# Down product of the sample rows: high and low halves of z in one stationary of 64 columns, and their units first in each group of the second block

## What is computed

```python
def ffn(h, w_up, w_down):
    return jnp.square(jax.nn.relu(h @ w_up)) @ w_down

xp = xp + ffn(rmsnorm(xp, norm_ffn_g[l]), w_up[l], w_down[l])
xs = xs + ffn(rmsnorm(xs, norm_ffn_g[l]), w_up[l], w_down[l])
...
y_prompt = rmsnorm(xp, norm_f_g)
y_sample = rmsnorm(xs, norm_f_g)
```

## Time and profile before

| | |
|---|---|
| median of 3 runs | 2716.34 us (2716.27 to 2719.45) |
| profiled execution | 2719.28 us, span 2717.6 us |
| mean granted clock of PE | 0.963 of full speed |
| busy | PE 2524.3, PEld 2268.7, DVE 1409.3, ACT 699.8, POOL 272.8 us |

### The profile page before, as it was taken

One profiled execution on the slowest core, in us unless ns is written; L12 is line 12 of the kernel. 1 busy time (PEld: TensorE's weight loads), 2 busy tenths in 40 slices (PEclk: granted clock), 3 DMA queues, 4 the chain that ended last, 5 costly groups with the idle time before them and its releaser, 6 DMA issues.

```text
span 2717.6 us, 36622 instructions
## 1 busy us (share of the span) xinstructions
PE 2524.3 (93%) x13872; PEld 2268.7 (83%) x13872; DVE 1409.3 (52%) x2411; ACT 699.8 (26%) x1421; POOL 272.8 (10%) x533
## 2 busy tenths in 40 slices
PE   5899999995699996489999999998799999999997
PEld 3799999995588885279898989897689888888986
DVE  5245654683566664454545454445544454445445
ACT  5223332211333431132121212123312121121212
POOL 4000011000333330210000000003400000000002
PEclk9999999997799997689999999999799999999999
DMA  4123334314455532232121111111312111111201
GB/s 140 42 71 99 102 113 124 114 62 146 143 148 147 141 111 69 85 117 62 32 62 31 62 34 59 41 52 40 116 32 62 31 46 46 46 46 31 62 23 70
DMA packets 212761, 208.03 MB, mean 77 GB/s; under 512 B 30251, under 2 KB 184043, under 8 KB 209322
## 3 DMA queue, kind: packets, MB, share of 16 engines
q1 hardware_dynamic: 212658, 206.63, 25.0%
HBM read 156.91 MB, written 49.79 MB: 76 GB/s over the span
## 4 chain that ended last, share of the span: by engine, by line
PE 53%; POOL 2%; issue 1%; ACT 1%; DMA 0%; DVE 0%; SPq 0%; DVEq 0%; POOLq 0%; ACTq 0%
PE bank L122 18%; PE bank L124 18%; PE bank L123 18%; ACT f_relu L140 0%; DMA f_up_raw<-in_w_up_dram 0%; PE bank L177 0%; POOL f_acc L1603 0%; POOL f_acc L1601 0%; POOL fn_rs L111 0%; POOL ff_rt L109 0%; POOL fn_ms L145 0%; POOL ff_rt L108 0%; POOL fn_rt L109 0%; POOL fn_rt L108 0%; POOL fn_rt L110 0%
## 5 line engine op out<-in xcount | busy, mean ns | idle before, releaser
L1710 DVE TENSOR_TENSOR f_acc<-bank,f_acc 128x512 f32<-128x512 f32 x512 | 353.2, 691 | 320.5 <-PE bank L124 319.9
L122 PE MATMUL bank<-f_h_hi,f_up_lo 128*128 128x344 f32 (+1 forms) x1536 | 494.3, 322 | 4.3 <-DVE f_up_lo L1705 2.2
L124 PE MATMUL bank<-f_h_hi,f_up_hi 128*128 128x344 f32 (+1 forms) x1536 | 492.6, 321 | 0.0
L123 PE MATMUL bank<-f_h_lo,f_up_hi 128*128 128x344 f32 (+1 forms) x1536 | 492.6, 321 | 0.0
L122 PE MATMUL bank<-f_dn_hi,f_z_lo 128*128 128x512 f32 x1088 | 432.8, 398 | 0.5 <-ACT f_relu L1638 0.5
L124 PE MATMUL bank<-f_dn_hi,f_z_hi 128*128 128x512 f32 x1088 | 429.6, 395 | 0.0
L123 PE MATMUL bank<-f_dn_lo,f_z_hi 128*128 128x512 f32 x1088 | 428.4, 394 | 0.0
L122 PE MATMUL bank<-h_hi,w_lo 128*128 128x412 f32 (+3 forms) x1000 | 352.7, 353 | 1.9 <-DVE w_lo L667 1.9
L123 PE MATMUL bank<-h_lo,w_hi 128*128 128x412 f32 (+3 forms) x1000 | 351.5, 352 | 0.0
L124 PE MATMUL bank<-h_hi,w_hi 128*128 128x412 f32 (+3 forms) x1000 | 351.1, 351 | 0.0
L122 PEld LDWEIGHTS bank<-f_h_hi,f_up_lo 128*128 128x128 f32 x1536 | 291.3, 190 | 7.7 <-DVE f_up_lo L1705 2.5
(11 more groups left out here) (326 smaller groups left out, 2918.1 us busy)
## 6 DMA issues: line engine op xcount, KB each, us to landing
f_up_raw<-in_w_up_dram SPq DMA_DIRECT2D x64, 512.0 KB, 4.8
f_dn_raw<-in_w_down_dram SPq DMA_DIRECT2D x64, 512.0 KB, 3.4
p_dram<-y SPq DMA_DIRECT2D x24, 1024.0 KB, 4.7
w_raw<-in_w_in_dram SPq DMA_DIRECT2D x24, 512.0 KB, 5.3
xres<-in_x_prompt_dram SPq DMA_DIRECT2D x16, 512.0 KB, 4.7
x_dram<-x SPq DMA_DIRECT2D x16, 512.0 KB, 3.1
f_acc<-x_dram SPq DMA_DIRECT2D x16, 512.0 KB, 4.8
out_y_prompt_dram<-f_acc SPq DMA_DIRECT2D x16, 512.0 KB
```

The costliest lines, as they stand in the source:

```text
L122: pe.matmul(out, wl, xh, start=start and k == 0, stop=False, skip_group_check=skip)
L123: pe.matmul(out, wh, xl, start=False, stop=False, skip_group_check=skip)
L124: last = pe.matmul(out, wh, xh, start=False, stop=stop and k == n - 1, skip_group_check=skip)
L1710: dve.tensor_tensor(dst, bank, dst, ALU.add).then_inc(s["y_added"], 1)
```

## The change

The stationary of the sample rows becomes `z_sample`, 64 columns wide for each j: columns 0 to 7 are the high part, columns 32 to 39 the low part, and the others are zero. One matmul (`both`) multiplies all 64 columns with the high part of `w_down`; a second one (`high`) multiplies the first 32 columns with its low part. So the unit's bank holds the high part's products in partitions 0 to 7 and the low part's in 32 to 39. DVE adds 64 partitions to an accumulator of 64 rows, `s_acc`. After the last group ACT moves rows 32 to 39 to `s_low`, DVE adds them to rows 0 to 7, and the rows are squared, scaled and stored. The two sample units are now the first two of each group of the second block. POOL makes their scales ahead of those of the prompt tiles. At the start of `ffn`, ACT zeroes the padding and saves the rows, DVE zeroes `s_acc`, and ACT puts the rows back. DVE makes `z_lo` of the sample columns with an instruction of its own.

```diff
...
-    z_hi = sb("z_hi", [P, GH, W], F32R)
-    z_lo = sb("z_lo", [P, GH, W], F32R)
+    z = sb("z", [P, GH, 2 * (BLK + PAD)], F32R)
+    z_hi, z_sample, z_lo = z[:, :, 0:W], z[:, :, BLK:BLK + 2 * PAD], z[:, :, BLK + 2 * PAD:]
+    s_acc = c.x_s_room
...
+    final_s = Stats(c, st, "ffs_", xn[:, 1, :])
+    s_low = xn[0:n, 0, :]
...
     def units(blk):
-        out = [(u, slice((u // 2) * P, (u // 2 + 1) * P), u % 2, psum[ZB + u % ZB][:, :],
-                slot(blk, u // 2)[:, (u % 2) * 512:(u % 2 + 1) * 512]) for u in range(2 * NBT)]
-        if blk == 1:
-            out += [(u, slice(BLK, W), u % 2, psum[ZB + u % ZB][0:n, :], c.x_s[:, (u % 2) * 512:(u % 2 + 1) * 512])
-                    for u in range(2 * NBT, UNITS[1])]
+        before = 2 * blk
+        out = sample_units() if blk == 1 else []
+        out += [(u + before, slice((u // 2) * P, (u // 2 + 1) * P), u % 2, psum[ZB + (u + before) % ZB][:, :],
+                 slot(blk, u // 2)[:, (u % 2) * 512:(u % 2 + 1) * 512]) for u in range(2 * NBT)]
         return out
+    def sample_units():
+        return [(u, None, u, psum[ZB + u][0:2 * PAD, :], s_acc[:, u * 512:(u + 1) * 512]) for u in range(2)]
...
+            eng.wait_ge(s["s_final"], 1)
+            eng.dma_start(io["y_sample"].rearrange("b s d -> (b s) d"), s_acc[0:n, :]).then_inc(s["s_stored"], 16)
             for m in range(NBT):
                 eng.wait_ge(stored[m % 2], 16 * (NBT // 2 + m // 2))
                 store_rows(1, m)
...
+            final_s.scales(pool, 0, 0, 1, NS)
             for pair in range(NBT // 2):
                 finals[1].scales(pool, pair, 2 * pair)
-            finals[1].scales(pool, NBT // 2, NBT, 1, NS)
...
+            act.activation(z_sample, heads(c.ident[:], GH), ACT.Copy, scale=0.0).then_inc(s["z_padded"], 1)
+            act.activation(s_low, c.x_s[:], ACT.Copy).then_inc(s["s_saved"], 1)
+            act.wait_ge(s["s_zeroed"], 1)
+            act.activation(c.x_s[:], s_low, ACT.Copy).then_inc(s["s_placed"], 1)
...
+            act.wait_ge(s["y_added"], outputs_before(1, NG - 1) + 3)
+            act.activation(s_low, s_acc[PAD:PAD + n, :], ACT.Copy).then_inc(s["low_moved"], 1)
+            act.wait_ge(s["s_summed"], 1)
+            final_s.square(act, 0, 0, s_acc[0:n, :], NS)
             for m in range(NBT):
                 finished_square(1, m)
...
+                        if cols.stop > BLK:
+                            ends = slice(BLK, W)
+                            dve.tensor_tensor(z_sample[:, j, PAD:PAD + n], sq[:, BLK - cols.start:], z_hi[:, j, ends].bitcast(F32), ALU.subtract)
+                        cols = slice(cols.start, min(cols.stop, BLK))
...
+            dve.wait_ge(s["s_saved"], 1)
+            dve.memset(s_acc[:], 0.0).then_inc(s["s_zeroed"], 1)
...
             for unit in units(1):
                 add(1, NG - 1, unit)
                 u = unit[0]
-                if u % 4 == 3 and u > 4:
-                    finish(1, (u - 7) // 2)
-                    finish(1, (u - 7) // 2 + 1)
+                if u == 3:
+                    dve.wait_ge(s["low_moved"], 1)
+                    dve.tensor_tensor(s_acc[0:n, :], s_acc[0:n, :], s_low, ALU.add).then_inc(s["s_summed"], 1)
+                elif u % 4 == 1 and u > 6:
+                    if u == 9:
+                        final_s.scaled(dve, 0, 0, s_acc[0:n, :], s_acc[0:n, :], fgain, NS).then_inc(s["s_final"], 1)
+                    finish(1, (u - 9) // 2)
+                    finish(1, (u - 9) // 2 + 1)
...
+            def down_sample(bank, js, cols, first, last):
+
+                for j in js:
+                    both = lambda: pe.matmul(bank, z_sample[:, j, :], dn_hi[:, j, cols], start=first and j == 0,
+                                             stop=last and j == GH - 1, skip_group_check=True)
+                    high = lambda: pe.matmul(bank[0:PAD, :], z_sample[:, j, 0:PAD], dn_lo[:, j, cols], start=False, stop=False,
+                                             skip_group_check=True)
+                    if j == 0:
+                        both()
+                        ins = high()
+                    else:
+                        high()
+                        ins = both()
+                return ins
...
```

More of the change, by code:

```diff
@@ L1462, in ffn @@
     W = BLK + n
+    PAD = 32
     ACCS = 12
@@ L1482, in ffn @@
     names = """up_loaded0 up_loaded1 dn_loaded up_hi_made up_lo_made dn_hi_made dn_lo_made z_ready relu_made zhi_made
-        sqr_made zlo_made y_ready y_added gain_loaded fgain_loaded""".split()
+        sqr_made zlo_made y_ready y_added gain_loaded fgain_loaded z_padded s_saved s_zeroed s_placed low_moved s_summed s_final s_stored""".split()
     s = {nm: sem("f_" + nm) for nm in names}
@@ L1581, in _ @@
                 store_rows(1, m)
-            eng.wait_ge(out_made[1], NBT + 1)
+            eng.wait_ge(s["s_stored"], 16)
             eng.wait_ge(stored[0], 16 * NBT)
-            eng.dma_start(io["y_sample"].rearrange("b s d -> (b s) d"), c.x_s[:]).then_inc(stored[0], 16)
-            eng.wait_ge(stored[0], 16 * NBT + 16)
             eng.wait_ge(stored[1], 16 * NBT)
@@ L1646, in finished_square @@
             def finished_square(blk, m):
-                act.wait_ge(s["y_added"], outputs_before(blk, NG - 1) + 2 * m + 3)
+                act.wait_ge(s["y_added"], outputs_before(blk, NG - 1) + 2 * blk + 2 * m + 3)
                 finals[blk].square(act, m, m, slot(blk, m))
@@ L1694, in _ @@
             act.wait_ge(s["zhi_made"], 2 * NTL * NZ)
+            act.wait_ge(s["y_added"], outputs_before(1, NG - 1) + 3)
+            act.activation(s_low, s_acc[PAD:PAD + n, :], ACT.Copy).then_inc(s["low_moved"], 1)
+            act.wait_ge(s["s_summed"], 1)
+            final_s.square(act, 0, 0, s_acc[0:n, :], NS)
             for m in range(NBT):
                 finished_square(1, m)
-            act.wait_ge(s["y_added"], outputs_before(1, NG) + 1)
-            finals[1].square(act, NBT, NBT, c.x_s[:], NS)
         @block.vector
@@ L1727, in group @@
                         dve.wait_ge(s["sqr_made"], q + 3)
-                        dve.tensor_tensor(z_lo[:, j, cols], sq, z_hi[:, j, cols].bitcast(F32), ALU.subtract).then_inc(s["zlo_made"], 1)
+                        if cols.stop > BLK:
+                            ends = slice(BLK, W)
+                            dve.tensor_tensor(z_sample[:, j, PAD:PAD + n], sq[:, BLK - cols.start:], z_hi[:, j, ends].bitcast(F32), ALU.subtract)
+                        cols = slice(cols.start, min(cols.stop, BLK))
+                        dve.tensor_tensor(z_lo[:, j, cols], sq[:, 0:cols.stop - cols.start], z_hi[:, j, cols].bitcast(F32),
+                                          ALU.subtract).then_inc(s["zlo_made"], 1)
                 if not last:
@@ L1747, in _ @@
             dve.wait_ge(s["gain_loaded"], 16)
+            dve.wait_ge(s["s_placed"], 1)
             normalise(0, 0)
@@ L1810, in down @@
                 cols = slice(half * 512, (half + 1) * 512)
+                if toks is None:
+                    return down_sample(bank, js, cols, first, last)
                 return three_pass(pe, bank, [(z_hi[:, j, toks], z_lo[:, j, toks], dn_hi[:, j, cols], dn_lo[:, j, cols]) for j in js],
                                   start=first, stop=last)
+            def down_sample(bank, js, cols, first, last):
[11 more added lines that the diff above has]
+                return ins
             def down_group(blk, gi, between=None):
@@ L1851, in first_block @@
                 up_block(blk * NTL, 0, zb[b])
+            pe.wait_ge(s["z_padded"], 1)
             pe.sem_inc(s["relu_made"], ZB)
@@ L1925, in build @@
         c.ident = keep.sb("ident", [P, P])
-        c.x_s = keep.sb("x_s", [NS, D])
+        c.x_s_room = keep.sb("x_s", [HALF, D])
+        c.x_s = c.x_s_room[0:NS, :]
         with ExitStack() as mixing:
```

1 line of the change is left out of this document (removed).

## The result

The changed kernel takes 2689.48 us, the median of 4 runs (2688.39 to 2690.70), against 2717.83 (2716.27 to 2719.45) for the kernel before, measured beside it: ratio 0.9894, 95% interval 0.9879 to 0.9910. The gain is 28.4 us. Forecast were 12.4 us and a time of 2703.9, with a range of 2700 to 2709. The profiled execution took 2690.70 us, its span 2689.0.

The account below looks back on a forecast made before the run. PE was taken to bound the kernel, by matmul count times spacing. 15 groups x 0.92 = 13.8 us gained less 1.4 lost in the tail is 12.4: 2716.3 - 12.4 = 2703.9 us, range 2700 to 2709.

Parts of the forecast that it names:

- What bounds the kernel: Second block: PE is busy all 690 us from 1960 to 2650, so time is number of matmuls times spacing.
- The spacing of what stays: Down product: a matmul costs its 512 moving columns, 0.230 us, however narrow the stationary; six take 1.39 us.
- 4 matmuls less, 0.92 a group: Second block's groups: two sample units save 4 matmuls of 0.230 us, period 47.79 to 46.87; sixteen groups give 14.7 us.
- The middle wait: Hand-over from j = 0 to j = 1 in a group: slack before z_lo falls from 0.73 to 0.18 us, nothing lost.
- Rival 3: Middle of each group: z_lo 0.3 us later than forecast, costing 2 to 3 us in all, 2706.3; chance 0.17.
- The start of ffn: Before the first square: copies and memset, at most 3.9 us, hidden behind a 5.9 us wait for memory; cost 0.
- The tail: After the last group's down product begins: sample chain first, DVE waits 1.8 us, PE stalls 1.6; end 1.4 us later.
- Rival 1: Tail: POOL and ACT 1.8 us quicker, no PE stall, tail gains 1.5 us; total gain 15.3, 2701.0; chance 0.15.
- rival 4: Tail: longer than computed by up to 3 us, its terms in series on POOL, 2707 us; chance 0.08.
- rival 2: Second block's groups: ten stationary width changes cost 0.17 us each, 14.8 us slower, 2731; chance 0.06 slower, 0.02 even.
- POOL held by DVE: Tail: DVE's 1.27 us scaling of the sample rows holds a POOL instruction of pair 0, adding 1.1 us.

Follow-up runs that it names:

- rooms alone: The kernel before, with room for 1088 columns instead of 1032 for each j of z_hi and z_lo: 2701.57 us, ratio 0.9934 to the kernel before.
- the run with three columns: The changed kernel, with the sample rows' scales made in one POOL batch with those of tiles 0 and 1: 2689.75 us.

## Why the prediction was wrong, by its own steps

1. **What bounds the kernel**: right. PE is busy all 680 us from 1960 to 2640 in the changed kernel too, and the time is a number of matmuls times a spacing.
2. **The spacing of what stays**: this step failed. The prediction took the spacing as a constant (0.230 in the gain, 1.39 for six matmuls in the tail) and multiplied only the 4 that go; a change of the spacing of the others stood in its sum at nothing, with no reason given. But the change moves three of the four pieces of z against the moving pieces (distances 32, 64 and 96 become 0), and with it the spacing of the 3072 matmuls of the down product with 128 stationary columns, from 0.233 to 0.227 in the mean. A single interval of the earlier trace rows, 2078.70 to 2078.93, had to stand for all of them: the mean over a whole second-block group was 0.2328 with 128 columns and 0.2302 with 8, a difference that asks for a reason, as does the gap to the 0.214 that 512 columns take by the 0.418 ns above (an estimate). The part of the change that brought 18.6 us (2720.15 to 2701.57, rooms alone) has no term in the sum.
3. **4 matmuls less, 0.92 a group**: 0.86 measured at like addresses. The narrow matmuls stand 0.2317 apart in the mean, as against 0.2267 in the kernel before with rooms of 1088; 8 of them in a group are the missing 0.04.
4. **The middle wait**: right, 0.18 us of slack forecast and measured. Rival 3 did not come.
5. **The start of ffn**: right. ACT's last copy ends 2.6 us before its first square, which waits for the rows from memory.
6. **The tail**: the chain was right in the links that were read (1.75 for 1.8, 1.4 for 1.6, the store ending the span 3.95 us after DVE for 4.1), the sum a little high: 0.9 us lost against the kernel before, 1.3 against it at like addresses, for 1.4. Rival 1 is out, and so is rival 4.
7. **Changes of width** (rival 2): they cost nothing that decides. Spacings of 0.23 to 0.24 at each change; at most the 5 ns of point 3, whose cause is open. The Trainium skill, "TensorEngine Tiling (Array Packing)", section "Key Properties", says that a change of tiling mode drains TensorE. If stationaries of 64 and 32 columns count as such modes, a drain would have shown as gaps, and this trace does not agree.
8. **POOL held by DVE**: right; POOL's instruction ran from 2661.99 to 2663.26 and DVE's from 2661.93 to 2663.19. The lock for one whole instruction that the Trainium skill describes in "SBUF — State Buffer", section "SBUF: two separate sides", fits this 1.27 us. The 3.05 us in the run with three columns is more than that: there POOL stayed held over three DVE instructions.

With the forecast's own terms, the change alone is 12.4 forecast and 10.5 (medians) to 11.6 (traces) measured. The other 18 us are a side effect of how a tensor was laid out.

What stays open: why the distance counts. In the slow kernels the intervals repeat from unit to unit without being equal (on average 238, 230, 230, 235, 232, 235 ns through the six matmuls of a unit before the change), and this even where every pair has the same distance (229 and 237 or 238 in turn at 128); in the fast ones all are 226 to 227. That looks like weight loads and moving reads getting in each other's way at some distances, but no run here shows the memory at work, so this is only argued. Nor is it shown which moving piece counts, the one that a stationary meets or the one that is read while it is loaded: `dn_hi` and `dn_lo` start alike in every kernel here. Not explained either is why the up product gains so much less.

## What to carry to other kernels

When a change declares a tensor anew, compare the start addresses of all stationary and moving pieces, and count the matmuls whose place changes, not only those that are added or removed. Where a PE-bound stretch has matmuls further apart than their columns need, and further than narrower ones, ask why before taking the spacing as a constant; here, rows padded to a multiple of 256 bytes gave 18.6 us for two edited lines. A chain moved ahead of others is best priced link by link in time order, with every queue it passes.

## What the runs showed of the hardware

- fp32r matmuls with 512 moving columns and a weight load each stand 0.2267 us apart when stationary and moving piece start alike within 256 bytes; 0.2289 at distance 192, 0.2333 at 128 and at 64 (the latter in rows at the start of a group), and 0.2318 to 0.2334 where distances are mixed. Moving both by 64 bytes changes nothing.
- With 320 to 384 moving columns the same brings only 0.8 ns on average, and 2.0 in the one block of 344.
- Stationaries of 128, 64 and 32 columns followed each other at 0.22 to 0.24 us without a gap.
- An instruction of POOL was held over several DVE instructions in a row: 3.05 us over three.
